# Key compression in a two-block transformer kernel: both groups side by side, rows read with a token's shift, positions as a bias, other places in the order

## What is computed

```python
idx = np.arange(n_cmp)[:, None] * STRIDE_CMP + np.arange(L_CMP)[None, :]   # 31 x 32
def compress(raw, pos, w1, w2):
    blk = raw[:, :, idx] + pos                   # groups x 31 x 32 x 64
    blk = blk.reshape(B, N_KV_GROUPS, n_cmp, L_CMP * HEAD_DIM)
    return jax.nn.silu(blk @ w1) @ w2            # w1: 2048 x 64, w2: 64 x 64
k_cmp = compress(k_cmp_raw, cmp_pos_k, phi_k_w1, phi_k_w2)
v_cmp = compress(v_cmp_raw, cmp_pos_v, phi_v_w1, phi_v_w2)
```

## Time and profile before

| | |
|---|---|
| median of 3 runs | 2471.18 us (2470.41 to 2475.91) |
| the profiled execution's own time | 2471.77 us |
| its span, first to last instruction | 2470.0 us |
| mean granted TensorE clock | 0.957 of 2.4 GHz |
| TensorE busy | 2265.8 us (92%) |
| VectorE, ScalarE, POOL busy | 1239.6, 994.0, 794.2 us |

### The profile page before, as it was taken

How to read it: one execution, slowest core, us unless ns; L and a number is a source line. 1 busy time by engine, 2 the same in 40 slices (tenths; PEclk the granted TensorE clock), 3 DMA queues, 4 the chain that set the end, 5 groups by cost and what they waited for, 6 DMA issues and landing times.

```text
span 2470.0 us, 31847 instructions
## 1 busy us (share of the span) xinstructions
PE 2265.8 (92%) x10614; PEld 1795.9 (73%) x10614; DVE 1239.6 (50%) x1917; ACT 994.0 (40%) x1630; POOL 794.2 (32%) x352
## 2 busy tenths in 40 slices
PE   3799999998789999959979999999899999999997
PEld 2677777776668888838847888888766657788886
DVE  6366666654353332259974333325467765333323
ACT  4433343333344432255544444222355554444322
POOL 2522222221444444420014444445111103444442
PEclk8999999998989999969989999999699999999999
DMA  3211101011212233201102222432100002222322
GB/s 123 94 35 35 42 34 42 34 37 60 91 60 93 96 103 104 89 26 52 59 17 86 101 93 96 140 104 80 35 18 17 17 9 68 94 93 93 106 97 78
DMA packets 43690, 169.96 MB, mean 69 GB/s; under 512 B 4848, under 2 KB 4976, under 8 KB 43120
## 3 DMA queue, kind: packets, MB, share of 16 engines
q1 hardware_dynamic: 43056, 163.82, 19.9%
q10 hardware_dynamic: 576, 5.37, 0.6%
HBM read 167.08 MB, written 2.10 MB: 68 GB/s over the span
## 4 chain that ended last, share of the span: by engine, by line
PE 79%; DVE 10%; issue 5%; ACT 4%; POOL 1%; DMA 1%; DVEq 1%; ACTq 0%; POOLq 0%; SPq 0%
PE bank L282 21%; PE bank L284 20%; PE bank L283 20%; PE bank L707 2%; PE bank L1727 2%; PE bank L699 1%; PE bank L712 1%; DVE ACC L382 1%; DVE act L778 1%; PE bank L1520 1%; ACT Pr L1778 1%; PE bank L1691 1%; POOL WL L247 1%; PE bank L1709 1%; PE bank L1279 1%
## 5 line engine op out<-in xcount | busy, mean ns | idle before, releaser
L247 POOL TENSOR_TENSOR WL<-raw,WR 128x1024 fp32r<-128x1024 f32 (+2 forms) x274 | 705.8, 2576 | 995.9 <-ACT WR L243 991.3
L282 PE MATMUL bank<-XR,WR 128*128 128x512 f32 x1528 | 629.9, 412 | 52.0 <-DVE XL L403 31.7
L284 PE MATMUL bank<-XR,WL 128*128 128x512 f32 x1528 | 603.3, 395 | 0.0
L283 PE MATMUL bank<-XL,WR 128*128 128x512 f32 x1528 | 602.3, 394 | 0.0
L243 ACT ACTIVATE WR<-raw 128x1024 fp32r<-128x1024 f32 (+2 forms) x230 | 256.2, 1114 | 731.5 <-PE bank L284 724.0
L282 PEld LDWEIGHTS bank<-XR,WR 128*128 128x128 f32 x1528 | 291.2, 191 | 129.0 <-issue 35.6
L282 PE MATMUL bank<-MR,WR 128*128 128x512 f32 (+1 forms) x856 | 338.7, 396 | 16.3 <-DVE ML L1444 7.6
L284 PEld LDWEIGHTS bank<-XR,WL 128*128 128x128 f32 x1528 | 291.1, 190 | 62.4
L283 PEld LDWEIGHTS bank<-XL,WR 128*128 128x128 f32 x1528 | 292.3, 191 | 59.3 <-issue 6.5
L283 PE MATMUL bank<-ML,WR 128*128 128x512 f32 (+1 forms) x856 | 334.4, 391 | 0.0
L284 PE MATMUL bank<-MR,WL 128*128 128x512 f32 (+1 forms) x856 | 333.9, 390 | 0.0
(11 more groups left out here) (285 smaller groups left out, 2835.1 us busy)
## 6 DMA issues: line engine op xcount, KB each, us to landing
raw<-w SPq DMA_DIRECT2D x224, 512.0 KB, 3.3
raw<-w SPq DMA_DIRECT2D x48, 704.0 KB, 4.1
raw<-w SPq DMA_DIRECT2D x16, 384.0 KB, 3.0
hT<-xT SPq DMA_DIRECT2D x1, 2048.0 KB, 8.0
hT<-xT ACTq DMA_DIRECT2D x1, 2048.0 KB, 8.1
phi<-phi ACTq DMA_DIRECT2D x1, 2048.0 KB, 10.0
out<-Y SPq DMA_DIRECT2D x8, 256.0 KB, 2.0
memT<-memT ACTq DMA_DIRECT2D x1, 1024.0 KB, 8.1
```

What stands on the lines that cost most here:

```text
L247: nc.gpsimd.tensor_tensor(WL[:, here], raw[:, here], WR[:, here].bitcast(F32), ALU.subtract).then_inc(weight_split, 1)
L282: nc.tensor.matmul(into, wr, xr(k0 + k), start=start, stop=False)
L283: nc.tensor.matmul(into, wr, xl(k0 + k), start=False, stop=False)
L284: mm = nc.tensor.matmul(into, wl, xr(k0 + k), start=False, stop=stop)
```

## The change

- **First layer.** `c_rows` now holds for each group (512 columns each) the rows on partitions 0 to 63 and the same rows one token later on 64 to 127. One matmul covers two positions of the window (128 rows) and both groups (62 moving columns, tokens 16 apart, read from `c_rows` directly): 2 networks x 16 matmuls instead of 2 x 2 x 32. `windows`, its memsets and additions go.
- **Positions.** Since the layer is linear, the positions are put through the same weights once (2 x 16 matmuls with one moving column) and added as the bias of the Silu. Four small copies make `pos_rows`, one copies the bias out of PSUM.
- **Evictions.** The two raw tiles are evicted by four operations of 64x512 each.
- **Places.** Bias products behind unit 1, first layers behind unit 3 (the fourth), second layer behind unit 6, then at once the unit of the first query pair, then the value transposes and gate transposes. VectorE and ScalarE get matching orders: Silu ahead of the keys, `q_scalar` and `q_vector` at the end of the kv functions, ahead of the distances and of the copies of turned values.
- **Keys.** VectorE makes four low parts instead of eight, and ScalarE copies them to the other partition half (`keys_twice`). `KC` holds both groups in one tile; phi2 has 64 rows and writes both halves.
- phi1 shrinks from 2 MB to 1 MB.

```diff
-        windows = [at(f"windows{i}", (32 + 4 * i) * KB, L_CMP * 32) for i in range(2)]
-        hidden = at("hidden", 40 * KB, 64)
-        KV_TILES = [c_rows[0], c_rows[1], k_rows[0], k_rows[1], v_rows[0], v_rows[1]]
-        phi2 = at("phi2", low + 8 * KB + 32, 2 * P)
+        c_rows = [at(f"c_rows{i}", (177 + 4 * i) * KB, 2 * SEQ) for i in range(2)]
+        hidden = at("hidden", behind_l + 4 * KB, P, parts=64)
+        hid_bias = at("hid_bias", behind_l + 5 * KB, 2, parts=64)
+        pos_rows = at("pos_rows", behind_l + 6 * KB, L_CMP)
...
+            def pair_weight(i, l):
+                at0 = (i * L_CMP // 2 + l) * 64
+                return phi1[:, at0:at0 + 64]
...
+                if j == 1:
+                    pe.wait_ge(pos_ready, 4)
+                    for i in range(2):
+                        for l in range(L_CMP // 2):
+                            col = i * L_CMP // 2 + l
+                            mm = nc.tensor.matmul(bank[7][0:64, i:i + 1], pair_weight(i, l), pos_rows[:, col:col + 1],
+                                                  start=l == 0, stop=l == L_CMP // 2 - 1)
+                    mm.then_inc(bias_done, 1)
+                if j == 3:
+                    pe.wait_ge(bias_ready, 2)
+                    for i in range(2):
+                        pe.wait_ge(rows_ready, 3 * i + 3)
+                        pe.wait_ge(tile_taken, seg_a.tile0 + i + 1)
+                        starts = c_rows[i][:, :].rearrange("p (g n s) -> p g n s", g=2, s=STRIDE)
+                        for l in range(L_CMP // 2):
+                            half, at0 = l // (STRIDE // 2), 2 * l % STRIDE
+                            mm = nc.tensor.matmul(HIDDEN_BANKS[i][0:64, 0:2 * N_CMP], pair_weight(i, l),
+                                                  starts[:, :, half:half + N_CMP, at0], start=l == 0, stop=l == L_CMP // 2 - 1)
+                        mm.then_inc(hid_done, 1)
             pe.wait_ge(input_ready, INPUT["q"] + DT)
-            pe.wait_ge(tile_taken, seg_a.tile0 + 3)
             products(pe, seg_a, seg_a.unit0 + 6, (seg_a.unit0 + 6) % 2, 0, kv_bank(6)[:, :],
                      lambda k: q_in_R[k], lambda k: q_in_L[k], True, True)
+            pe.wait_ge(phi2_loaded, 16)
+            pe.wait_ge(hid_ready, 2)
+            for g in range(2):
+                mm = nc.tensor.matmul(bank[7][:, g * 32:(g + 1) * 32], phi2[:, 0:P], hidden[:, g * 32:(g + 1) * 32], start=True, stop=True)
+            mm.then_inc(cmp_done, 1)
+            for g in range(2):
+                mm = nc.tensor.matmul(bank[2][0:32, g * 64:(g + 1) * 64], hidden[:, 64 + g * 32:64 + (g + 1) * 32], phi2[:, P:P + 64],
+                                      start=True, stop=True)
+            mm.then_inc(cmp_done, 1)
+            pair_tensor(pe, 0, 0)
             for i in range(2):
-                pe.wait_ge(tile_taken, seg_a.tile0 + 6)
+                pe.wait_ge(tile_taken, seg_a.tile0 + 5 + i)
                 for b in range(NB):
                     mm = nc.tensor.transpose(bank[3 + i][:, b * P:(b + 1) * P], v_rows[i][:, b * P:(b + 1) * P], ident)
                 mm.then_inc(vt_turned, 1)
-            pe.wait_ge(phi2_loaded, 16)
-            pe.wait_ge(tile_taken, seg_a.tile0 + 7)
-            for i in range(2):
-                pe.wait_ge(windows_ready, 2 * i + 2)
-                for g in range(2):
-                    rows = slice(64 * g, 64 * g + 64)
-                    for l in range(L_CMP):
-                        w = phi1[rows, (i * L_CMP + l) * 64:(i * L_CMP + l + 1) * 64]
-                        mm = nc.tensor.matmul(bank[5 + i][rows, 0:32], w, windows[i][rows, l * 32:(l + 1) * 32],
-                                              start=l == 0, stop=l == L_CMP - 1)
-                mm.then_inc(hid_done, 1)
...
-                mm = nc.tensor.transpose(bank[2][:, b * 48:(b + 1) * 48], g_rows[0:48, b * P:(b + 1) * P], ident[0:48, 0:48])
+                mm = nc.tensor.transpose(bank[6][:, b * 48:(b + 1) * 48], g_rows[0:48, b * P:(b + 1) * P], ident[0:48, 0:48])
             mm.then_inc(gate_turned, 1)
-            pe.wait_ge(hid_ready, 2)
-            nc.tensor.matmul(bank[7][:, 0:32], phi2[:, 0:P], hidden[:, 0:32], start=True, stop=True)
-            nc.tensor.matmul(bank[6][0:32, 128:256], hidden[:, 32:64], phi2[:, P:2 * P], start=True, stop=True).then_inc(cmp_done, 1)
...
             act.wait_ge(unit_done, seg_a.unit0)
             for n in range(DT):
                 act.wait_ge(q_scaled, n + 1)
                 nc.scalar.activation(q_in_R[n], cols(SQ, n % 2), ACT.Identity).then_inc(input_high, 1)
+            for i in range(2):
+                act.wait_ge(hid_done, i + 1)
+                into = hidden[:, i * 64:(i + 1) * 64].rearrange("p (g n) -> p g n", g=2)[:, :, 0:N_CMP]
+                from_ = HIDDEN_BANKS[i][0:64, 0:2 * N_CMP].rearrange("p (g n) -> p g n", g=2)
+                nc.scalar.activation(into, from_, ACT.Silu, bias=hid_bias[:, i:i + 1]).then_inc(hid_ready, 1)
             act.wait_ge(unit_done, seg_a.unit0 + 6)
             for i in range(2):
                 act.wait_ge(tile_taken, seg_a.tile0 + 3 + i)
                 for g in range(2):
                     for rows in (HALF[g], HALF[1 - g]):
                         nc.scalar.activation(KS[i][g][0][rows, :], k_rows[i][HALF[g], :], ACT.Identity).then_inc(keys_high, 1)
+            for i in range(2):
+                for g in range(2):
+                    act.wait_ge(keys_low, 2 * i + g + 1)
+                    nc.scalar.activation(KS[i][g][1][HALF[1 - g], :], KS[i][g][1][HALF[g], :].bitcast(F32), ACT.Identity).then_inc(keys_twice, 1)
             act.wait_ge(tile_taken, seg_a.tile0 + 7)
             nc.scalar.activation(g_rows[0:48, :], g_rows[0:48, :], ACT.Sigmoid).then_inc(gate_sig, 1)
-            for i in range(2):
-                act.wait_ge(hid_done, i + 1)
-                nc.scalar.activation(hidden[:, i * 32:(i + 1) * 32], bank[5 + i][:, 0:32], ACT.Silu).then_inc(hid_ready, 1)
             act.wait_ge(cmp_done, 1)
-            for g in range(2):
-                for rows in (HALF[g], HALF[1 - g]):
-                    nc.scalar.activation(KC[g][0][rows, :], bank[7][HALF[g], 0:32], ACT.Identity).then_inc(cmp_high, 1)
+            nc.scalar.activation(KC[0][:, :], bank[7][:, 0:64], ACT.Identity).then_inc(cmp_high, 1)
+            q_scalar(act, 0, 0)
...
+            V.memset(hidden[:, :], 0.0).then_inc(bias_ready, 1)
+            for i, name in enumerate(("pos_k", "pos_v")):
+                for q in range(2):
+                    first = PARAMS[name][0]
+                    pos = params[HALF[q], first:first + L_CMP].rearrange("p (l q) -> p q l", q=2)[:, q]
+                    V.tensor_copy(pos_rows[HALF[q], i * L_CMP // 2:(i + 1) * L_CMP // 2], pos).then_inc(pos_ready, 1)
...
+            def rows_of(i):
+
+                for g in range(2):
+                    into = c_rows[i][:, g * SEQ:(g + 1) * SEQ]
+                    for q in range(2):
+                        ins = V.tensor_tensor(into[HALF[q], 0:SEQ - q], kv_bank(i)[HALF[g], q:SEQ], R[HALF[g], q:SEQ], ALU.mult)
+                        ins.then_inc(tile_taken if g and q else rows_ready, 1)
+
             q_scale(0)
             q_scale(1)
             for j in range(6):
                 dve.wait_ge(unit_done, seg_a.unit0 + j + 1)
-                V.tensor_tensor(KV_TILES[j][:, :], kv_bank(j)[:, :], R[:, :], ALU.mult).then_inc(tile_taken, 1)
+                if j < 2:
+                    rows_of(j)
+                    if j:
+                        dve.wait_ge(bias_done, 1)
+                        V.tensor_copy(hid_bias[:, :], bank[7][0:64, 0:2]).then_inc(bias_ready, 1)
+                else:
+                    V.tensor_tensor(KV_TILES[j][:, :], kv_bank(j)[:, :], R[:, :], ALU.mult).then_inc(tile_taken, 1)
                 for n in range(2 * j, 2 * j + 2):
                     if n < DT:
                         q_low(n)
                         if n + 2 < DT:
                             q_scale(n + 2)
             for i in range(2):
-                dve.wait_ge(tile_taken, seg_a.tile0 + i + 1)
-                order.link(V.memset(windows[i][:, :], 0.0))
-                out_w = windows[i][:, :].rearrange("p (l n) -> p l n", l=L_CMP)
-                rows = c_rows[i][:, :].rearrange("p (n s) -> p s n", s=STRIDE)
-                for half in range(2):
-                    pos = params[:, PARAMS["pos_k" if i == 0 else "pos_v"][0] + half * STRIDE:][:, 0:STRIDE]
-                    V.tensor_tensor(out_w[:, half * STRIDE:(half + 1) * STRIDE, 0:N_CMP], rows[:, :, half:half + N_CMP],
-                                    over_columns(pos, N_CMP), ALU.add).then_inc(windows_ready, 1)
+                for g in range(2):
+                    dve.wait_ge(keys_high, 4 * i + 2 * g + 1)
+                    V.tensor_tensor(KS[i][g][1][HALF[g], :], k_rows[i][HALF[g], :], KS[i][g][0][HALF[g], :].bitcast(F32),
+                                    ALU.subtract).then_inc(keys_low, 1)
```

(76 more changed lines are left out.)

1 line of the change is left out of this document (removed).

## The result

The changed kernel takes 2446.73 us (median of 4 runs, 2445.6 to 2448.93) against 2473.55 (median of 4, 2470.41 to 2477.91), a ratio of 0.9891 with a 95% interval of 0.9872 to 0.9911. The forecast was 2445.2 with a range of 2441 to 2454. So the time was right; the profile shows that two of the terms behind it were not: the price of the networks and the gain behind the pair unit.

The account below looks back on a forecast made before the run. TensorE bounds the kernel (79% of the chain), by waits, small products and half clock in the kvq stage. 36.3 us go, 10.3 come, +1.0 and -1.0 behind: net 26.0 off 2471.77, median 0.6 lower: 2445.2, range 2441 to 2454.

Parts of the forecast that it names:

- What goes (36.3): From the seventh unit's end to the pair unit's start 34.07 us, plus 2.21 in the pair unit, leave TensorE's path.
- Networks (3.9): First-layer matmuls behind the fourth unit: 64 records at 0.061 us each, 3.9 us.
- The upper end: High price of a small record, 0.111 us as in L1683: 7.1 us for the networks' 64 records.
- rival 1: Networks and bias cost near 0.111 us a record, moving columns being 64 bytes apart: +6.4, 2451.6 us; chance 0.18.
- Bias (3.9): Position products behind the second unit: 64 records at 0.061 us each, 3.9 us.
- the fall of the clock behind it (1.7): After the bias records, one stretch of 3.41 us at half clock, losing 1.7 us.
- No wait ahead of bias, networks or unit 7: TensorE's own additional 9.5 us cover VectorE's additional 4.2 us, with 5.6 us to spare ahead of unit 7.
- Second layer (0.8): Ahead of the pair unit: eight records at 0.11 us and less, with the hand-over 0.8 us.
- Behind the pair unit (+1.0): First dense scores wait for VectorE's copies, starting 4.05 us after the pair unit's end instead of 3.03: +1.0.
- The gain of 1.0: Transposes fill part of the hole behind the pair unit, so its half-clock stretch goes, at six chances in ten: -1.0.
- the loss of 1.7: What the old half-clock stretch of 1779.98 to 1783.39, behind the pair unit, lost in all: 1.7 us.
- Sum: Whole path: 36.3 goes, 10.3 comes, +1.0 and -1.0 behind the pair unit; net 26.0 us saved.

Follow-up runs that it names:

- the repeated profile: A second profile of the changed kernel, with nothing changed; its stage from the norm's sum to the first dense scores was 57.25 us again.
- the twelve profiles of the new order: All profiles of the changed kernel and its follow-up variants: seven with the bias records, five without them.
- the second 22.6: A second set of rounds, the unaltered changed kernel timed against the kernel before: 2448.95 against 2471.55 us.

## Why the prediction was right, point by point

- **What goes (36.3): right in size, half right in cause.** The gap, the 256 records and the slow pair unit went. But "the idle gap also let the clock fall: the networks run wholly at 0.50" named the wrong cause for most of it. Without the gap the old records ran at 0.50 all the same from 4.1 us after their start.
- **Networks (3.9): the step that failed.** "I take 0.061" set the reading of columns 64 bytes apart at nothing. Measured 6.97, 3.1 more. The upper end, 7.1, held it, and rival 1 had named the mechanism; it set TensorE's price by VectorE's ratio too high (0.25 a record) and by L1683 nearly right (0.111). For adjacent columns 0.060 is exact.
- **Bias (3.9): right**, 3.83, and the fall of the clock behind it (1.7) too, 1.8 by the run without bias.
- **No wait ahead of bias, networks or unit 7: right.** VectorE's last low part of a query input (L1563 before, L1594 after) ended 28.5 us after the norm's sum against 27.6 before (1728.9 - 1701.32); I had allowed 4.4 more. The longer evictions were mostly made up: the sixteen operations on the query inputs took 17.9 us together against 21.8. Those of over 2 us among them lie beside a subtraction of POOL (L247), three in this stretch against four before.
- **Second layer (0.8): right**, 0.90.
- **Behind the pair unit (+1.0): right**, 4.29 from the unit's end to the scores against 4.05 worked out (its four parts add to 4.00) and 3.03 before. ScalarE had 1.9 us to spare ahead of the pair unit's end against 1.8 worked out.
- **The gain of 1.0 from a clock that holds: not had in the profiled execution**, where 3.41 us at 0.50 remain; in the repeated profile the clock did hold. The sum took the loss of 1.7 at six chances in ten. That chance was too high: the stretch came in ten of the twelve profiles of the new order. The Trainium skill, page TensorE: Matmul & The Clock Gate, section PE-mode transpose, says that transposes don't count as busy for the clock. By that rule the stretch would stay: the profiled execution agrees, the repeated one does not.
- **Sum.** At the first dense scores the working gives 25.0 (26.0 with the gain of 1.0, which falls behind them); measured 21.1. Of the missing 3.9, 3.1 are the networks, 0.25 the hole, 0.1 the second layer; the rest is not traced. The whole still came out at 26.0, as the stretches ahead and behind were 4.9 shorter in this execution than in the one before. Both differ between executions of one kernel: the norm's sum starts at 1699.24 in this profile and at 1701.39 in the repeated one. So the close agreement is partly luck. The first medians are 26.8 apart, the second 22.6, nearer to the stage's 21.1.
- The placement, which I counted as free and did not price, brings 0.3 us. The evictions in four operations and the copies of the keys on ScalarE were not run by themselves; the profile only shows no wait of TensorE for them.

## What to carry to other kernels

Lay a matmul's moving operand out so that columns read one after the other lie side by side; for small fp32 products a gather by 16 bytes or more nearly doubled their time, and a VectorE eviction that is needed anyway can write the order that TensorE reads. A bias that comes from the same weights is cheaper as one more moving column than as matmuls of its own, which here cost 3.83 us of records and then 1.8 of clock. Compare two kernels by the length of the changed stage between fixed events in the profile; totals that contain a loop of small products, as here, carry several us that differ with the clock from execution to execution.

## What had not been expected of the hardware

- fp32 matmul records with 64 weight columns and 62 moving ones at full clock: 0.060 us adjacent, 0.061 every second column, 0.114 every fourth, 0.109 every sixteenth.
- With one moving column instead of 62 a record costs the same 0.060 us, and PEld is busy for 3.81 of the 3.83 us; with 128 weight columns and 32 moving ones it was 0.111. So the weight load seems to set the price.
- The clock can fall with TensorE busy throughout: over the old first-layer records it was busy for 4.13 of 4.13 us, at 0.99 to 1.00, and then the granted clock was 0.50 to the end of the records.
